# One block for a whole two-model, four-layer program: layer boundaries without loop, barriers and semaphore clears

## Chip, cores, metric

One NeuronCore of a Trainium2 chip. The metric is the device time of one execution in microseconds; smaller is better.

## What is computed

Two transformer-like blocks in sequence on one sequence of 256 tokens with 1024 features, each block two layers deep, all in f32:

```python
def first_block(x, ...):
    for l in range(DEPTH):                      # DEPTH = 2
        h = rms_norm(x, norm_mix_pre[l])
        mix = hybrid_mixer(h, w_in[l], ...)      # SSM, two softmax attentions, one top-k attention, gates
        x = x + rms_norm(mix, norm_mix_post[l])
        h = rms_norm(x, norm_ffn_pre[l])
        x = x + rms_norm(swiglu(h, w_ffn_in[l], w_ffn_out[l]), norm_ffn_post[l])
    return x

def second_block(x, mem, positions, ...):
    for l in range(DEPTH):
        h = rmsnorm(x, norm_mix[l])
        x = x + mixer_block(h, positions, w_in[l], ...)   # MLA, spatial gate, GLA, delta net, gates
        x = x + cross_attention(rmsnorm(x, norm_xattn[l]), rmsnorm(mem, norm_mem[l]), ...)
        x = x + squared_relu_mlp(rmsnorm(x, norm_mlp[l]), w_up[l], w_down[l])
    return rmsnorm(x, norm_final)
```

Every layer reads its own weights once; they are most of the data.

## The kernel before

`build` loads `x` and shared constants, then calls `first_block` and `second_block`. Tiles of the first have names with `a_`, of the second with `b_`. Each has a loop over its two layers that is executed on the chip (`nc.Fori`), so the program holds one copy of a layer's instructions for each block. In the loop stands one block (`nc.Block`) with one instruction stream for each engine, written out by hand: TensorE (PE), ScalarE (ACT), VectorE (DVE), GpSimd (POOL) and SyncE (SP), which issues every DMA. Engines meet only through semaphores.

A layer is a **stream of weight parts**, 87 in a layer of block 1 and 84 in one of block 2, most of 1 MB. For part `h` SP loads it into one of three slots of `ring`; ACT's `hi` (L707, L2198) rounds it to the matmul's input type into `whi`; DVE's `lo` (L923, L2462) writes the rest into `wlo`; and PE multiplies three times (lo by hi, hi by lo, hi by hi), at L400, L660 and L690 in block 1 and L1675, L1701, L1752 and L2181 in block 2. There are three slots of each: SP waits for `lo_ok` of part `h - 3`, ACT for PE to have used part `h - 3`.

The activations are split in the same way. Before each large product stands a **turn**: ACT squares `x` and sums, DVE makes the mean square, POOL the power -1/2, DVE scales `x` into `xm` (L937, L2476; the tile is named `probs`), PE turns it in 16 small products (L390, L1666), ACT writes `nhi` and DVE `nlo`, and then the first matmul of the product can start. It happens at the start of each layer (L710 on) and again in the middle (`norm_in(3, ...)` in block 1, `norm_in(6, ...)` and `norm_in(7, ...)` in block 2). At the end of a layer comes the down projection (`dn`, parts from `H_DN` or `H_DN2`); its result is normed and added to `x` in block 1 (`norm_out`, L946 and L948) and added in block 2 (`residual`, L2810).

At the end of a layer all engines meet, the semaphores are cleared and they meet again:

```python
            nc.all_engine_barrier()
            for s in sems:
                nc.gpsimd.sem_clear(s)
            nc.all_engine_barrier()
```

Only then does SP issue the next layer's loads: the parameter rows `par` (L346: 6 DMAs; L1604: 8), which PE turns (L581, L2123) and DVE copies to `parT`, the first parts (L356, L1636), and small tensors (L359: 4; `smalls`: 11 in block 2). Between the blocks stands another block of its own: SP loads `con2` and `pos`, DVE works out angles in a chain of dependent steps (L1566 to L1576), ACT takes their sine (L1583). After block 2 one more block does the last norm (L3007 to L3030), and a last one writes the output (L3063). At the start `build` waits for `x` and the constants, then `first_block` for `con1`, in blocks of their own.

Of the kernel before, what the change touches and what calls it, by code (L numbers as in the profile page):

```python
# [1 line left out]

# [14 lines left out]
P = 128  # L17
# [68 lines left out]

W1 = 512
# [52 lines left out]
def first_block(nc, ps, x, con, bfc, a):  # L140
    with ExitStack() as ctx:

        place = [29056]

        def at(name, shape, dt=F32, offset=None):

            size = int(np.prod(shape[1:])) * (2 if dt == BF16 else 4)
            if offset is None:
                offset = place[0]
                place[0] = (offset + size + 31) // 32 * 32  # L150
            return nc.alloc_sbuf_tensor_at("a_" + name, shape, dt, offset=offset)

        def sem(name):
            s = ctx.enter_context(nc.semaphore("a_" + name))
            sems.append(s)
            return s

        sems = []
        ident = con[:, C_ID:C_ID + P]
        ident_bf, maskT_bf, maskQ_bf = (bfc[:, i, :] for i in range(3))  # L160
        tri = con[:, C_U:C_U + NT * SEQ].rearrange("p (t l) -> p t l", t=NT)
        maskQ = con[:, C_MQ:C_MQ + P]

        con1 = at("con1", [P, N_CONST1])
        cos, sin = con1[:, C1_COS:C1_COS + SEQ], con1[:, C1_SIN:C1_SIN + SEQ]
        rot = con1[:, C1_ROT:C1_ROT + P]
        ring = at("ring", [P, SLOTS, PART])
        whi, wlo = at("whi", [P, SPLITS, PART], F32R), at("wlo", [P, SPLITS, PART], F32R)
        nhi, nlo = at("nhi", [P, KD, SEQ], F32R), at("nlo", [P, KD, SEQ], F32R)

        base = place[0]
        gates = at("gates", [P, 32, SEQ])
        hid = gates
        dump = at("dump", [P, NT, D], offset=base)
        xbcp = at("xbcp", [P, 8, SEQ + 4], offset=base)
        xbc = at("xbc", [P, 8, SEQ], offset=base + 8320)
        xd = at("xd", [P, 2, NT, W1], offset=base + 16512)
        y = at("y", [P, NT, W1], offset=base + 24704)

        base = place[0]
        ys = at("ys", [P, 4, 4, SEQ])
        rl = at("rl", [P, 4, 384], offset=base + 8192)
        hhi, hlo = (at(n, [P, SPLITS, 2 * SEQ], F32R, offset=base + i * 6144) for i, n in enumerate(("hhi", "hlo")))

        base = place[0]
        fq, fk, fv = at("fq", [P, 4, SEQ]), at("fk", [P, 4, SEQ]), at("fv", [P, NT, W1])
        dq, dk, dv = fq, fk, fv  # L190
        merged = at("merged", [P, KD, SEQ], offset=base)

        base = place[0]
        mq, mk, mv = at("mq", [P, 4, SEQ]), at("mk", [P, 4, SEQ]), at("mv", [P, NT, W1])
        sc8 = at("sc8", [P, 8, 384], offset=base + 4096)
        ahi, alo = (at(n, [P, 4, SEQ], F32R, offset=base + i * 4096) for i, n in enumerate(("ahi", "alo")))
        gpost2 = at("gpost2", [P, D], offset=base + 8192)
        probs = at("probs", [P, 8, SEQ])
        xm = probs[:, :, :].rearrange("p (t a) b -> p t (a b)", t=NT)  # L200

        base = place[0]
        pT = at("pT", [P, 8, SEQ])
        iqf = at("iqf", [P, 4, SEQ], offset=base)
        cb = at("cb", [P, 2, 384], offset=base + 4096)
        bhi, blo = (at(n, [P, 4, SEQ], F32R, offset=base + i * 4096) for i, n in enumerate(("bhi", "blo")))

        base = place[0]  # L210
        z = at("z", [P, NT, W1])
        gpost1 = at("gpost1", [P, D], offset=base)
        ffg = at("ffg", [P, 2, 2 * SEQ], offset=base)
        o = z
        rt = at("rt", [P, 2, SEQ])
        par, parT = at("par", [NPAR1, P]), at("parT", [P, NPAR1])
        small = at("small", [P, 4, 8])
        sel, nsel = at("sel", [P, 16], F32R), at("nsel", [P, 16], F32R)
        iw = at("iw", [P, NT, 4])
        sp = at("sp", [P, 6, NT * 16])  # L220
        lcat = at("lcat", [P, NT, P])
        asg = at("asg", [P, 16])
        cumS = at("cumS", [P, SEQ], F32R)
        ncum = at("ncum", [P, NT, 16])
        isc = at("isc", [P, 384])
        pen = at("pen", [P, 384], BF16)
        top8 = at("top8", [P, 8])
        nmx, rsum, rinv = at("nmx", [P, 2, 8]), at("rsum", [P, 2, 8]), at("rinv", [P, 8])
        ssq, msq, rstd = (at(n, [P, 5, 4]) for n in ("ssq", "msq", "rstd"))
        nhalf = at("nhalf", [P, 4])  # L230
        assert place[0] <= 229344, place[0]

        dst = dict(xbc=xbcp[:, :, 3:SEQ + 3], iqk=iqf, few=iqf[:, 2:4, :],
                   fq=fq, fk=fk, fv=fv, mq=mq, mk=mk, mv=mv, dq=dq, dk=dk, dv=dv, z=z)
        isct = [isc[:, 0:P], isc[:, P:3 * P]]
        pent = [pen[:, 0:P], pen[:, P:3 * P]]
        rlt = [rl[:, :, 0:P], rl[:, :, P:3 * P]]

        con1_in = sem("con1_in")
        par_in, small_in, gpost_in = sem("par_in"), sem("small_in"), sem("gpost_in")  # L240
        landed = [sem(f"landed{i}") for i in range(SLOTS)]
        hi_ok, lo_ok = sem("hi_ok"), sem("lo_ok")
        full, turn_ps, free_a, free_v = (sem(n) for n in ("full", "turn_ps", "free_a", "free_v"))
        par_ps, par_ok = sem("par_ps"), sem("par_ok")
        ssq_ok, msq_ok, rstd_ok = sem("ssq_ok"), sem("msq_ok"), sem("rstd_ok")
        xn_ok, x_ok, tr_ps, nhi_ok, nlo_ok = (sem(n) for n in ("xn_ok", "x_ok", "tr_ps", "nhi_ok", "nlo_ok"))
        conv_ok, silu_ok, init_ok = sem("conv_ok"), sem("silu_ok"), sem("init_ok")
        few_ps, spv, spe, rope_ok = (sem(n) for n in ("few_ps", "spv", "spe", "rope_ok"))
        lcat_ok, cum_ps, cum_ok = sem("lcat_ok"), sem("cum_ps"), sem("cum_ok")
        cb_ps, cb_ok, xs_ps, xs_ok = sem("cb_ps"), sem("cb_ok"), sem("xs_ps"), sem("xs_ok")  # L250
        dec_ps, dec_ok, sc_ok = sem("dec_ps"), sem("dec_ok"), sem("sc_ok")
        y_ps, y_free, yt_ok, yt_ps, yt_out = sem("y_ps"), sem("y_free"), sem("yt_ok"), sem("yt_ps"), sem("yt_out")
        ix_ps, ix_rl, isc_ok, pen_ok = sem("ix_ps"), sem("ix_rl"), sem("isc_ok"), sem("pen_ok")
        qk_ps, mx_ok, ex_ok, pt_ps = sem("qk_ps"), sem("mx_ok"), sem("ex_ok"), sem("pt_ps")
        pt_a, pt_v, o_ps, o_ok, ot_ps, ot_ok = (sem(n) for n in ("pt_a", "pt_v", "o_ps", "o_ok", "ot_ps", "ot_ok"))
        sig_ok, yh_ok, yl_ok = sem("sig_ok"), sem("yh_ok"), sem("yl_ok")
        pr_ps, pr_free, mg_ok, mh_ok, ml_ok = (sem(n) for n in ("pr_ps", "pr_free", "mg_ok", "mh_ok", "ml_ok"))
        out_used, mix_ps, half_used = sem("out_used"), sem("mix_ps"), sem("half_used")
        fg_free, fu_free, hh_ok, hs_ok, dn_ps = (sem(n) for n in ("fg_free", "fu_free", "hh_ok", "hs_ok", "dn_ps"))
        dch = sem("dch")  # L260

        def cols(src, l, c, n):
            return src[bass.ds(l, 1), :, c:c + n].rearrange("a (k p) c -> p (a k) c", p=P)

        def rows(src, l, r, k):
            return src[bass.ds(l, 1), r:r + k * P, :].rearrange("a (k p) c -> p (a k) c", p=P)

        def branch_rows(l, n, j):
            return a["w_branch"][bass.ds(l, 1), n].rearrange("a (k p) c -> p (a k) c", p=P)[:, :, 512 * j:512 * j + 512]

        H_GATE = N_IN1
        H_BR = H_GATE + N_GATE1
        H_OUT = H_BR + 8
        H_FIN = H_OUT + 4
        H_DN = H_FIN + 2 * (HID1 // 256)
        H_END = H_DN + KH1 // 2
        parts = [(8, n, lambda l, c=c, n=n: cols(a["w_in"], l, c, n)) for c, n, _ in IN1]
        parts += [(8, 256, lambda l, c=c: cols(a["w_gate"], l, 256 * c, 256)) for c in range(N_GATE1)]
        parts += [(4, 512, lambda l, n=n, j=j: branch_rows(l, n, j)) for n in range(4) for j in range(2)]  # L280
        parts += [(2, D, lambda l, i=i: rows(a["w_out"], l, 2 * i * P, 2)) for i in range(4)]
        parts += [(8, 256, lambda l, c=c, j=j: cols(a["w_ffn_in"], l, HID1 * j + 256 * c, 256))
# [25 lines left out]
        def last_fill(i):  # L308
            return filled["in", i, len(IN1[i][2]) - 1] if i < N_IN1 else filled["gate", i - N_IN1]
# [2785 lines left out]
```

## Time and profile before

| | us |
|---|---|
| median of 3 runs | 2556.69 (2553.71 to 2557.05) |
| the profiled execution, its own time | 2554.51 |
| its span, first to last instruction | 2552.4 |
| PE busy in the span | 2371.9 |
| DVE, ACT, POOL busy | 1431.7, 1093.0, 48.5 |
| mean granted TensorE clock | 0.968 |

The span is what the trace shows; the execution's own time is 2.1 us more. "Boundary" below is the stretch from the last matmul of one layer to the first full matmul of the next: the first is between the layers of block 1, the second between the blocks, the third between the layers of block 2.

### The profile page before, as it was taken

To read this page: it belongs to the slowest core of one execution; us is meant where nothing else is said; L and a number is where in the kernel's file an instruction comes from. 1 tells how busy PE (TensorE), PEld (TensorE's weight loads), DVE (VectorE), ACT (ScalarE), POOL (GpSimd) and SP (SyncE) were. 2 spreads that over 40 slices of the span, in tenths; PEclk is the share of its full clock that TensorE was granted. 3 is DMA by queue.
4 is the path that set the end of the run, shared out by engine and by line. 5 is a ranking of instruction groups with operands and counts; after the bars stand their busy time and mean duration, and the time that the engine had idled before them with its cause. 6 is when DMAs were issued, how large, how long until landed. Compare 5 with 4: busy or idle time off the path is not lost. (4 is left out here: it accounts for less than half of the span.)

```text
span 2552.4 us, 40497 instructions
## 1 busy us (share of the span) xinstructions
PE 2371.9 (93%) x17164; PEld 2216.8 (87%) x17164; DVE 1431.7 (56%) x1573; ACT 1093.0 (43%) x1356; POOL 48.5 (2%) x49
## 2 busy tenths in 40 slices
PE   6999998998799999899759999989987999998996
PEld 6988997997798899799659998979966999897985
DVE  6555457444655545644447867454545876744553
ACT  4534444333453354434246433543424643443442
POOL 0000000000000000000000000000000000000000
PEclk9999999999899999999979999999998999998998
DMA  6523355543743336555254434445526443444552
GB/s 201 159 83 110 114 191 165 180 169 114 200 139 93 102 114 198 165 168 197 92 161 125 126 100 146 158 149 165 183 98 188 130 119 100 158 140 148 182 194 78
DMA packets 300001, 370.32 MB, mean 145 GB/s; under 512 B 25006, under 2 KB 267300, under 8 KB 299812
## 3 DMA queue, kind: packets, MB, share of 16 engines
q1 hardware_dynamic: 299812, 367.62, 45.8%
q8 instruction: 140, 2.29, 0.4%
q14 instruction: 49, 0.40, 0.0%
HBM read 366.55 MB, written 1.05 MB: 144 GB/s over the span
## 5 line engine op out<-in xcount | busy, mean ns | idle before, releaser
L400 PE MATMUL ps<-a_nhi,a_wlo 128*128 128x256 f32 x1792 | 525.0, 293 | 12.7 <-DVE a_nlo L953 11.2
L400 PE MATMUL ps<-a_nlo,a_whi 128*128 128x256 f32 x1792 | 508.0, 284 | 0.0
L400 PE MATMUL ps<-a_nhi,a_whi 128*128 128x256 f32 x1792 | 507.9, 283 | 0.0
L923 DVE TENSOR_TENSOR a_wlo<-a_ring,a_whi 128x2048 fp32r<-128x2048 f32 x174 | 395.6, 2286 | 108.3 <-ACT a_whi L707 107.8
L2462 DVE TENSOR_TENSOR b_wlo<-b_ring,b_whi 128x2048 fp32r<-128x2048 f32 (+1 forms) x168 | 379.6, 2263 | 136.2 <-ACT b_whi L2198 136.0
L707 ACT CAST a_whi<-a_ring 128x2048 fp32r<-128x2048 f32 x174 | 331.1, 1905 | 195.3 <-PE ps L400 73.2
L1675 PE MATMUL ps<-b_nhi,b_wlo 128*128 128x256 f32 x1296 | 378.4, 292 | 16.1 <-DVE b_wlo L2462 8.5
L2198 ACT CAST b_whi<-b_ring 128x2048 fp32r<-128x2048 f32 (+1 forms) x168 | 316.2, 1884 | 165.8 <-PE ps L2181 77.4
L1675 PE MATMUL ps<-b_nlo,b_whi 128*128 128x256 f32 x1296 | 369.8, 285 | 0.0
L1675 PE MATMUL ps<-b_nhi,b_whi 128*128 128x256 f32 x1296 | 369.7, 285 | 0.0
L400 PEld LDWEIGHTS ps<-a_nhi,a_wlo 128*128 128x128 f32 x1792 | 345.3, 193 | 18.9 <-DVE a_wlo L923 12.2
L400 PEld LDWEIGHTS ps<-a_nlo,a_whi 128*128 128x128 f32 x1792 | 344.7, 192 | 2.5 <-issue 2.4
L400 PEld LDWEIGHTS ps<-a_nhi,a_whi 128*128 128x128 f32 x1792 | 344.2, 192 | 0.0
L1675 PEld LDWEIGHTS ps<-b_nhi,b_wlo 128*128 128x128 f32 x1296 | 251.9, 194 | 19.2 <-DVE b_wlo L2462 9.4
L1675 PEld LDWEIGHTS ps<-b_nlo,b_whi 128*128 128x128 f32 x1296 | 252.0, 194 | 0.9 <-issue 0.5
L1675 PEld LDWEIGHTS ps<-b_nhi,b_whi 128*128 128x128 f32 x1296 | 251.6, 194 | 0.0
L2181 PE MATMUL ps<-b_whi,b_hlo 128*128 128x512 f32 x256 | 99.6, 389 | 0.0
L2181 PE MATMUL ps<-b_wlo,b_hhi 128*128 128x512 f32 x256 | 99.6, 389 | 0.0
L2181 PE MATMUL ps<-b_whi,b_hhi 128*128 128x512 f32 x256 | 99.6, 389 | 0.0
L1244 DVE TENSOR_TENSOR a_gates<-a_ffg,ps 128x512 f32<-128x512 f32 x22 | 15.1, 688 | 142.5 <-PE ps L400 142.5
L775 ACT ACTIVATE a_probs<-ps,a_nmx 128x128 f32<-128x128 f32 (+1 forms) x96 | 39.3, 430 | 94.5 <-DVE a_nmx L1074 94.5
L421 PE MATMUL ps<-a_wlo,a_nhi 128*128 128x256 f32 x256 | 75.6, 295 | 0.0
(537 smaller groups left out, 4390.0 us busy)
## 6 DMA issues: line engine op xcount, KB each, us to landing
a_ring<-in_w_in SPq DMA_DIRECT2D x50, 1024.0 KB, 5.2
b_ring<-in_w_in SPq DMA_DIRECT2D x50, 1024.0 KB, 6.1
a_ring<-in_w_ffn_in SPq DMA_DIRECT2D x44, 1024.0 KB, 5.4
a_ring<-in_w_gate SPq DMA_DIRECT2D x32, 1024.0 KB, 5.3
b_ring<-in_w_up SPq DMA_DIRECT2D x32, 1024.0 KB, 5.5
b_ring<-in_w_down SPq DMA_DIRECT2D x32, 1024.0 KB, 5.0
a_ring<-in_w_ffn_out SPq DMA_DIRECT2D x22, 1024.0 KB, 5.0
a_ring<-in_w_branch SPq DMA_DIRECT2D x16, 1024.0 KB, 5.1
```

The costliest lines, as they stand in the source:

```text
L400: mm = T.matmul(out, w[:, k, c:c + P], x_[:, k, :], start=k == 0 and n == 0, stop=k == KD - 1 and n == 2)
L421: mm = T.matmul(b[:, t * size:(t + 1) * size], x_[:, k, t * P:(t + 1) * P], w[:, k, c:c + size], start=k == 0 and j == 0, stop=k == KD - 1 ...
L707: S.copy(part(whi, h), part(ring, h)).then_inc(hi_ok, 1)
L775: ins = S.activation(probs[:, s, 0:w], L[:, s, 0:w], ACT.Exp, bias=nmx[:, n % 2, s:s + 1], accum_out=rsum[:, n % 2, s:s + 1])
L923: V.tensor_tensor(part(wlo, h), part(ring, h), part(whi, h).bitcast(F32), ALU.subtract).then_inc(lo_ok, 1)
L1244: V.tensor_tensor(hid[:, 2 * c:2 * c + 2, :], ffg[:, c % 2, :].rearrange("p (b c) -> p b c", b=2), ps[:, 4 + c % 2, :].rearrange("p (b c) ...
L1675: mm = T.matmul(out, w[:, k, c:c + P], x_[:, k, :], start=k == 0 and n == 0, stop=k == KD - 1 and n == 2)
L2181: mm = T.matmul(ps[:, 4 + 2 * t + half, :], hidden_of(x_, i)[:, kk, t * P:(t + 1) * P], w[:, kk, half * 512:(half + 1) * 512], start=i + k ...
L2198: A.copy(part(whi, h), part(ring, h)).then_inc(hi_ok, 1)
L2462: V.tensor_tensor(part(wlo, h), part(ring, h), part(whi, h).bitcast(F32), ALU.subtract).then_inc(lo_ok, 1)
```

## The change

All engines' work is put into one block. Each layer becomes a `Stage`, and the engines run through four stages that are written out one after the other; there is no loop, no barrier between them and no clearing. Semaphores count on through the program: `Counting` adds what the earlier layers have given to every wait (`GAINED_1`, `GAINED_2`), and the two blocks share semaphores and the same addresses for `ring`, `whi`, `wlo`, `nhi`, `nlo`. At the end of a layer, `hi`, `lo` and SP go on with the first parts of the next layer; its `par` rows are loaded at part `H_DN + 1` and turned by PE in the down projection (`i == 6` or `i == 9`). The angles of block 2 are worked out by DVE at `H_DN + 6` of the layer before (`set_vector`), the sines by ACT at `H_DN + 8`. `x` is loaded in two halves, each with its semaphore; the last norm and the output go by halves, and `norm_final` is loaded during the last down projection.

The core of the diff, without the change of indentation:

```diff
+    def wait_ge(self, sem, n):
+        self.engine.wait_ge(sem, n + self.done[sem.name])
...
-        with nc.Fori(0, DEPTH) as l:
-            with nc.Block() as block:
...
+    def ends(l):
+        at_ = lambda sem, n: (sem, n + earlier(l, 0)[sem.name])
+        return Ends(split=[at_(lo_ok, H_END - 2 + i) for i in range(3)],
+                    used=[at_(*used[H_END - 3]), at_(*used[H_END - 2]), at_(dn_ps, 2)],
+                    x=[at_(x_ok, 3), at_(x_ok, 4)], hidden=at_(hs_ok, KH1 // 2))
...
+            elif prior is not None:
+                sp_.wait_for(*prior.split[h])
+            if h == H_DN + 1:
+                following.params(sp_.engine, following.layer)
+            if l == 0 and h == 1:
+                sp_.dma_start(con1[:, :], a["constants_1"]).then_inc(con1_in, 16)
...
-                    pe.wait_ge(par_in, 96)
-                    T.transpose(ps[:, 4, 0:NPAR1], par[:, :], ident[0:NPAR1, 0:NPAR1]).then_inc(par_ps, 1)
                     turned(0)
...
+            if i == 6:
+                pe.wait_ge(fu_free, KH1 // 2)
+                following.params_turn(pe.engine, following.layer, 4)
...
+        def hi(h):
+            if h < H_END:
+                split_hi(act.engine, l, h, prior)
+            elif following is not None:
+                following.split_hi(act.engine, following.layer, h - H_END, ends(l))
...
                     for t in range(NT):
+            act.wait_for(*(x_in[t] if prior is None else prior.x[t]))
                         squares(0, t, x[:, t, :])
+        if prior is None:
                     hi(0)
...
+            if i == H_DN + 6:
+                following.set_vector(dve.engine, following.layer)
+            if i == H_DN + 7:
+                following.params_out(dve.engine, following.layer, 4)
...
-            nc.all_engine_barrier()
-            for s in sems:
-                nc.gpsimd.sem_clear(s)
-            nc.all_engine_barrier()
...
                         if h == SLOTS - 1:
+                sp_.wait_for(*prior.hidden)
+                sp_.wait_for(init_ok, 2)
                             smalls()
...
+            if i == 9 and following is not None:
+                following.params_turn(pe.engine, following.layer, 2)
...
+        if following is None:
+            for t in range(NT):
+                sp_.wait_for(y_ok, t + 1)
+                sp_.dma_start(y.rearrange("a (t p) d -> p (a t) d", p=P)[:, t, :], x[:, t, :]).then_inc(y_done, 16)
```

How the instructions move on ACT at the second boundary. Before, from the last casts of block 1's layer to the first of block 2's (`a_hhi` is the hidden activation's rounded half, `b_trig` the sines):

```order
L707 CAST a_whi<-a_ring 128x2048 [waits a_landed2,a_half_used]
L905 CAST a_hhi<-a_gates 128x512 [waits a_fu_free]
L710 ACTIVATE a_dump,a_ssq<-ps 128x1024 [waits a_dn_ps] x2
L336 UNCONDITIONAL_BRANCH
L335 REGISTER_ALU [waits barrier_Pool_Activation_PE_DVE_SP_release]
L335 COMPARE_AND_BRANCH
L1580 UNCONDITIONAL_BRANCH
L1583 ACTIVATE b_trig<-b_lnp 32x256 [waits b_ang_ok]
L1584 ACTIVATE b_trig<-b_lnp 32x256
L1544 UNCONDITIONAL_BRANCH [waits b_trig_ok]
L1588 UNCONDITIONAL_BRANCH [waits barrier_Pool_Activation_PE_DVE_SP_release]
L2189 UNCONDITIONAL_BRANCH
```

and now:

```order
L804 CAST a_whi<-a_ring 128x2048 [waits landed2,half_used]
L1741 ACTIVATE b_trig<-b_tmp_148 32x256 [waits ang_ok]
L1742 ACTIVATE b_trig<-b_tmp_148 32x256
L1017 CAST a_hhi<-a_gates 128x512 [waits fu_free]
L2354 CAST b_whi<-b_ring 128x1536 [waits landed0,half_used]
L2354 CAST b_whi<-b_ring 128x1536 [waits landed1,half_used]
L818 ACTIVATE a_dump,a_ssq<-ps 128x1024 [waits dn_ps] x2
L2368 ACTIVATE b_dump,b_ssq<-x 128x1024 [waits x_ok] x2
L2374 ACTIVATE b_nhi<-ps,b_parT 128x256 [waits tr_ps,par_ok]
```

The branches and barrier waits are gone; the next block's first two casts stand ahead of the last squares of this one, and the squares of `x` follow on `x_ok` alone.

On DVE at the same place, now, the set-up chain of block 2 inside block 1's down projection:

```order
L1025 TENSOR_TENSOR a_wlo<-a_ring,a_whi 128x2048 [waits hi_ok]
L1720 MEMSET b_nhalf 128x8
L1721 MEMSET b_eps 128x1
L1722 MEMSET b_wg 128x128
L1724 CAST b_tmp_148<-b_pos 32x256 [waits con1_in]
...
L1734 TENSOR_SCALAR b_tmp_148<-b_tmp_148 32x256 [waits dch]
L1392 TENSOR_TENSOR a_hlo<-a_gates,a_hhi 128x512 [waits hh_ok]
L1025 TENSOR_TENSOR a_wlo<-a_ring,a_whi 128x2048 [waits hi_ok]
L2627 COPY b_parT<-ps 128x63 [waits par_ps]
```

`a_hlo` is what PE's next down-projection part waits for; the chain of ten dependent steps now stands ahead of it, where before it stood in a block of its own.

On SP (L128 is the helper that issues), now, what is issued between the last parts of block 1 and the fourth part of block 2:

```order
L128 DMA b_ring<-in_w_in 128x4x384 [waits lo_ok] x2
L128 DMA b_ring<-in_w_in 128x8x64 [waits lo_ok]
L128 DMA b_ring<-in_w_in 128x8x32 x2
L128 DMA b_sgw<-in_sg_w 128x4x128 [waits init_ok,hs_ok]
L128 DMA b_wuq<-in_mla_w_uq 128x2x384
...
L128 DMA b_lnp<-in_sg_ln_b 128x256
L128 DMA b_ring<-in_w_in 128x8x256 [waits lo_ok] x17
```

The order of the loads is that of before; their waits are now on the layer before (`lo_ok`, and `hs_ok` for the small tensors), not on a barrier.

## Rows read from the trace of the kernel before

**Rows 1.** The page: part 1 (busy time), part 3 (queue that brings instructions).

```profile
PE 2371.9 (93%) x17164; PEld 2216.8 (87%) x17164; DVE 1431.7 (56%) x1573; ACT 1093.0 (43%) x1356; POOL 48.5 (2%) x49
...
q8 instruction: 140, 2.29, 0.4%
```

**Rows 2.** Waits of PE: engine, line, on whom; total us, times, longest.

```profile
PE ps L2123 <- DMA b_par<-in_dn_conv: 60.3, 2, 37.1
...
PE ps L1675 <- DVE b_wlo L2462: 8.5, 4, 5.6
```

**Rows 3.** Timeline of PE, first boundary: start us, us, engine, line, operation [idle].

```profile
628.95 0.39 PE L690 MATMUL ps<-a_whi,a_hhi 128*128 128x512 f32 x1
...
646.49 0.41 PE L581 MATMUL ps<-con,a_par 92*128 92x92 f32 x1 [17.16 <-DMA a_par<-in_norm_ffn_pre]
...
655.89 0.55 PE L400 MATMUL ps<-a_nhi,a_wlo 128*128 128x256 f32 x1 [4.04 <-DVE a_nlo L953]
```

**Rows 4.** Timeline inside layer 1 of block 1, PE and DVE.

```profile
430.21 0.39 PE L660 MATMUL ps<-a_whi,a_nhi 128*128 128x512 f32 x1
...
434.75 1.23 DVE L948 TENSOR_TENSOR x<-x,a_probs 128x1024 f32<-128x1024 f32 x1
...
438.44 0.75 DVE L937 TENSOR_SCALAR a_probs<-x,a_rstd 128x1024 f32<-128x1024 f32 x1 [0.44 <-POOL a_rstd L1265]
...
442.39 0.36 PE L400 MATMUL ps<-a_nhi,a_wlo 128*128 128x256 f32 x1 [0.74 <-DVE a_nlo L953]
```

**Rows 5.** Timeline of PE and DVE, second boundary (block 1 to block 2).

```profile
1260.42 0.39 PE L690 MATMUL ps<-a_whi,a_hhi 128*128 128x512 f32 x1
...
1276.50 0.28 DVE L1566 CAST b_lnp<-b_pos 32x256 f32<-32x256 int32 x1 [3.76 <-DMA b_pos<-in_positions]
...
1279.96 0.28 DVE L1576 TENSOR_SCALAR b_lnp<-b_lnp 32x256 f32<-32x256 f32 x1
...
1302.70 0.41 PE L1701 MATMUL ps<-b_whi,b_nlo 128*128 128x384 f32 x1 [0.89 <-DVE b_nlo L2482]
```

**Rows 6.** Timeline of DVE and PE, third boundary.

```profile
1904.35 1.22 DVE L2810 TENSOR_TENSOR x<-x,ps 128x1024 f32<-128x1024 f32 x1 [1.50 <-PE ps L2181]
...
1932.20 0.66 PE L1701 MATMUL ps<-b_whi,b_nlo 128*128 128x384 f32 x1 [0.79 <-DVE b_nlo L2482]
```

**Rows 7.** Stretches (us; busy of PE, PEld, DVE, ACT, POOL; PEclk, DMA, GB/s), PE's timeline.

```profile
442.00:444.00 2.00, 1.61 (x13) 1.63 (x14) 2.00 (x6) 1.98 (x6) 0.00 (x0) 1.00 0.03 8
...
1722.21 0.55 PE L1675 MATMUL ps<-b_nhi,b_wlo 128*128 128x256 f32 x1 [3.00 <-DVE b_nlo L2482]
...
1728.00:1732.00 4.00, 4.00 (x34) 4.00 (x34) 0.49 (x1) 1.12 (x2) 0.00 (x0) 0.97 0.27 93
...
1936.00:1938.00 2.00, 2.00 (x12) 2.00 (x11) 1.62 (x2) 0.00 (x0) 0.00 (x0) 0.88 0.38 97
```

**Rows 8.** Timeline of the start: SP's DMA issues, DVE, PE.

```profile
6.97 0.50 DVE L3053 CAST bfc<-con 128x128 bf16<-128x128 f32 x3 [6.97 <-DMA x<-in_x]
...
11.32 0.37 SPq L346 DMA_DIRECT2D a_par<-in_norm_mix_pre  x1
...
14.01 2.41 SPq L356 DMA_DIRECT2D a_ring<-in_w_in  x3
...
24.38 0.55 PE L400 MATMUL ps<-a_nhi,a_wlo 128*128 128x256 f32 x1 [5.62 <-DVE a_nlo L953]
```

**Rows 9.** Timeline of the end: DVE, SP.

```profile
2529.43 1.22 DVE L2810 TENSOR_TENSOR x<-x,ps 128x1024 f32<-128x1024 f32 x1 [1.50 <-PE ps L2181]
...
2544.98 2.48 DVE L3023 SCALAR_TENSOR_TENSOR x<-x,b_rstd,b_probs 128x1024 f32<-128x1024 f32 x2 [1.50 <-DMA b_probs<-in_norm_final]
2547.95 0.39 SPq L3063 DMA_DIRECT2D out<-x  x1
```

**Rows 10.** Timeline of ACT and DVE near the end of layer 1.

```profile
613.05 1.91 ACT L707 CAST a_whi<-a_ring 128x2048 fp32r<-128x2048 f32 x1 [3.01 <-PE ps L690]
...
617.21 0.69 DVE L1253 TENSOR_TENSOR a_hlo<-a_gates,a_hhi 128x512 fp32r<-128x512 f32 x1
```

More of the change, by code:

```diff
@@ L1 @@
 from contextlib import ExitStack
+from dataclasses import dataclass
 import numpy as np
@@ L84, in column, with __init__, wait_for, dma_start @@
     return ap.broadcast_to([ap.shape[0], n])
+@dataclass
+class Ends:
+    split: list
+    used: list
+    x: list
+    hidden: tuple
+@dataclass
+class Stage:
+    layer: int
+    params: object
+    params_turn: object
+    params_out: object
+    set_vector: object
+    set_picks: object
+    set_scalar: object
+    split_hi: object
+    split_lo: object
+    sync: object
+    tensor: object
+    scalar: object
+    vector: object
+    gpsimd: object
+    ends: Ends
+class Counting:
+    def __init__(self, engine, done):
+        self.engine, self.done = engine, done
+    def wait_ge(self, sem, n):
+        self.engine.wait_ge(sem, n + self.done[sem.name])
+    def wait_for(self, sem, n):
+        self.engine.wait_ge(sem, n)
+    def dma_start(self, *args):
+        return self.engine.dma_start(*args)
@@ L3039, in build @@
         con_in, con_bf = (ctx.enter_context(nc.semaphore(n)) for n in ("con_in", "con_bf"))
-        out_done = ctx.enter_context(nc.semaphore("out_done"))
+        x_in = [(ctx.enter_context(nc.semaphore(f"x_in{t}")), 16) for t in range(NT)]
+        sems, n_chain = {}, [0]
+        stages = first_block(nc, ctx, sems, n_chain, ps, x, x_in, con, bfc, a)
+        stages += second_block(nc, ctx, sems, n_chain, ps, x, con, bfc, a, y)
+        first = stages[0]
+        run = [(s, stages[i - 1].ends if i else None, stages[i + 1] if i + 1 < len(stages) else None)
+               for i, s in enumerate(stages)]
         with nc.Block() as block:
```

5155 lines of the change are left out of this document (2623 added, 2532 removed).

## Prediction

> **What bounds the kernel now.** I began with the page. PE is busy 93% of the span [rows 1], and every other engine has slack, so the question is where PE stands still. The view of its waits answers that [rows 2]: its longest waits are for `b_par`, the parameter rows of a layer of block 2, 60.3 us in two waits. Those rows are loaded only after the barrier, so this is a layer boundary seen from PE. I then went through PE's timeline and noted every idle time above 0.4 us. Apart from some of about 1 us they lie at five kinds of place: the start, the three boundaries, the end, the norm in the middle of a layer, and a wait for `b_wlo` soon after a boundary. So the time is a dense stream of matmuls plus these gaps, and each gap can be priced from the timeline.
>
> The gaps, from the last matmul of a layer to the first full one of the next:
> - first boundary [rows 3]: 628.95 + 0.39 = 629.34 to 655.89, 26.55 us;
> - second [rows 5]: 1260.42 + 0.39 = 1260.81 to 1302.70, 41.89 us;
> - third [rows 6]: DVE's last addition to `x` starts at 1904.35, the first matmul at 1932.20, 27.85 us.
>
> **What a boundary costs without barriers.** Nothing has to be guessed here, since the middle of a layer in block 1 has the same chain: squares of the product, norm, addition to `x`, squares of `x`, norm, turn, `nhi`, `nlo`, matmul, with its weights split beforehand. From its last matmul (430.21 + 0.39 = 430.60) to the next at 442.39 it takes 11.79 us [rows 4]. From the end of the last addition to `x` (434.75 + 1.23 = 435.98) to the matmul it is 6.41 us [rows 4]. I take these as what remains.
>
> **The sum**, against the profiled execution's own time, 2554.5 us:
> - First boundary: the chain is the one of rows 4. 26.55 - 11.79 = 14.8 us saved.
> - Second: the same chain, with block 2's turn at its end. 41.89 - 11.79 = 30.1 us. The set-up of block 2 that stood here goes elsewhere, below.
> - Third: block 2 only adds to `x`; the addition ends at 1904.35 + 1.22 = 1905.57, and 6.41 us later, at 1911.98, the matmul can start. 1932.20 - 1911.98 = 20.2 us.
> - Weights behind a boundary: PE waits 8.5 us in four waits for `b_wlo` [rows 2], of which the largest, 5.6, and one of 2.0 stand behind the second and third boundary, where the fourth part was loaded after 11 small tensors. Now these loads stand before the boundary, some 10 us earlier than their use. 7.6 us.
> - Start: the first weight part is issued at 14.01 and PE's first full matmul comes 10.37 us later [rows 8]. Now the three loads of `x` and constants are issued at once from about 0.7 us, and the six `par` loads (11.32 to 14.01, so 0.45 us each [rows 8]) follow directly: 0.7 + 9 x 0.45 = 4.8 us for the first part, matmul at 4.8 + 10.4 = 15.2 instead of 24.38. 9.2 us. The other input is not later: `x` had landed by 6.97 [rows 8], and the norm and the turn of `x` fit in the 8 us that are left.
> - End: before, addition to `x` until 2529.43 + 1.22 = 2530.65, last scaling until 2544.98 + 2.48 = 2547.46, output issued at 2547.95, span end 2552.4 [rows 9]. Now the second half is squared, normed and scaled right behind its addition. From an addition's end to the scaling's start is 438.44 - 435.98 = 2.46 us [rows 4], one scaling is 1.24: 2530.65 + 2.46 + 1.24 = 2534.35, plus the 4.94 us from there to the end of the span as before, 2539.3. 13.1 us.
> - PE's three turns of `par` stood in idle time, and stand now in the middle of a down projection: 3 x 0.41 us [rows 3] on PE. -1.2 us.
> Together 93.8 us.
>
> **What is hidden.** DVE's chain for the angles lasts 1279.96 + 0.28 - 1276.50 = 3.7 us, with its memsets 4 us [rows 5]. It now stands ahead of an `a_hlo`. A part of the down projection lasts (629.34 - 613.05) / 3 = 5.43 us. With ACT's cast at 613.05, `a_hlo` is done at 617.90 [rows 10], while the matmuls that need it start two parts after 613.05, at 623.9. So DVE has 6 us to spare, and 4 us fit; it makes the delay good in the next parts, of whose 5.4 us it uses 3.0. If that cover is gone, the cost is at most 4 us, once. ACT's two sines are shorter and have the same cover. SP's additional loads (10, 6 and 8 small ones, 3 to 5 us of issuing at each boundary) stand ahead of a weight part that is loaded three parts, 16 us, before its use. The clears and barriers themselves were on POOL and in the idle time already counted. Waits of SP on `hs_ok` hold back only the small tensors and the fourth part, by less than one part.
>
> **The clock.** After an idle time the granted clock is at 0.50 (1.2 GHz) for a while, then 1.00 (2.4 GHz). At the third boundary it is 0.88 over 1936 to 1938 [rows 7], so it rose at about 1936.5: 4.3 us at half speed, 2.1 us lost; I take as much for the other two, 6.3 us in all. What the shorter gaps will cost is open, since the rows differ: after the 11.8 us gap in block 1 the clock is 1.00 from the first matmul on (442 to 444), while after the like gap in block 2 it is 0.97 only from 1728 on and the matmuls began at 1722.21 [rows 7], so 5.9 us at half speed, 2.9 us lost. The bounds for each boundary are 0 and 2.9; I take the middle, as neither row is nearer to all three: 3 x 1.45 = 4.3. Net gain 2.0 us.
>
> The Trainium skill, "TensorE: Matmul & The Clock Gate", section "HAM oscillation — how this bites in real kernels", says that an idle gap between bursts of matmuls takes the clock back to half, so that each burst starts cold. By this rule all three boundaries would pay in full, and the sum would be 4.3 us worse than mine; the row of 442 to 444 does not agree with it, that of block 2 does.
>
> Sum: 93.8 + 2.0 = 95.8, so 2554.5 - 95.8 = 2458.7 us. The median of the runs stands 2.2 us above the profiled execution; the forecast for the median is thus between 2458.7 and 2460.9, and I give **2459.5**.
>
> **Rivals.**
> - Every burst starts cold, 2463.8 us: the mechanism is the idle time of 8 to 12 us that is left at each boundary; it decides if the clock has fallen when the first matmul comes. For it speaks the gap in block 2, against it the one in block 1, whose chain the first two boundaries share. This is the case that the Trainium skill, "TensorE: Matmul & The Clock Gate", would have.
> - The work that crosses the boundaries gets in the way: the chain on DVE makes a part late (4 us), the 11 small loads hold the fourth part back at two boundaries as long as today (7.6 us), and the three groups of `par` loads delay a weight part by their issue (24 x 0.45 = 11 us). In full 23 us are given back, about 2482 us. Rows 10 speak against it, with 6 us of slack per part where the additions are 4.
> - The boundaries don't close as written, because some wait counts on what comes late (a slot, a semaphore of the layer before): at all three boundaries about half of the 65 us stays, 2492 us. The order of the instructions on ACT and DVE speaks against it.
> - Slower than before: the program is twice as long, since no layer's code is used twice. The queue for instructions brought 140 packets with 2.29 MB [rows 1]. If the longer program made PE wait for its instructions, at each such packet, the price that decides is 95.8 / 140 = 0.7 us per packet; at 1 us each it gives 2554.5 - 95.8 + 140 = 2599 us. Against it: PE's timeline shows no idle time of that kind in a layer's 600 us, where it too runs straight on, and the packets are already as many as the instructions executed, not as those in the program.
>
> **How the numbers follow.** Something over 0.2% (5 us) is what a measurement of this kernel can tell from no change. My forecast has a chance of 0.6, cold bursts 0.2, the crossing work 0.12, boundaries half open 0.05, slower 0.02; some 0.01 is left for no change. So faster 0.97, same 0.01, slower 0.02. The range: at the low end all boundaries are warm (4.3 us), the two norms in block 2 too because their phase has moved (2 x 2.9), and half-size transfers at start and end save 1 us each, 2447.6. At the high end everything is cold (4.3), the first part lands behind `x` and constants (2.2 us: 6.97 plus the 5.2 us from issue to landing instead of 10.0), and the wait of 5.6 us stays: 2471.6; a little of the crossing work makes it 2474. The rest of it and the other rivals lie outside.
>
> **What would show it.** The profile of the changed kernel should have: gaps of 11.5 to 12 us at the first two boundaries and 7.5 to 8 at the third, ended by `nlo`, not by a DMA; no wait of 5.6 us for `b_wlo`; the first full matmul at 15 to 16 us; 10 us from the last matmul to the end; PE busy the same within 10 us; down projections without idle time on PE. I would be wrong if a gap is ended by `par` or by a landing part, if PE waits for `b_wlo` or `a_hlo` in a down projection, or if small idle times without a releaser are spread over the stream.

## The result, and the profile after

| | before | changed |
|---|---|---|
| median of the runs, us | 2556.22 (4 runs) | 2452.61 (2452.03 to 2454.24, 4 runs) |
| ratio, 95% interval | | 0.9595 [0.9583, 0.9606] |
| profiled execution, own time | 2554.51 | 2452.11 |
| its span | 2552.4 | 2450.2 |
| PE busy in the span | 2371.9 | 2364.6 |
| PE idle (span less busy) | 180.5 | 85.6 |

The forecast was 2459.5 us with a range of 2447.6 to 2474: right in direction and inside the range, 6.9 us too high. The last two lines of the table carry the reading: PE executes the same 17164 matmuls and now idles 94.9 us less; being busy with them takes 7.3 us less, most of it because fewer of them run at half speed (below).

The page after, the first line, part 1 and the instruction queue of part 3:

```profile
span 2450.2 us, 38959 instructions
...
PE 2364.6 (97%) x17164; PEld 2210.0 (90%) x17164; DVE 1430.4 (58%) x1564; ACT 1090.3 (44%) x1353; POOL 49.8 (2%) x50
...
q8 instruction: 136, 2.23, 0.4%
```

The waits of PE after (engine, line, on whom; total us, times, longest), against [rows 2]:

```profile
PE ps L486 <- DVE a_probs L1078: 24.1, 4, 7.5
PE ps L1822 <- DVE b_probs L2656: 20.7, 4, 7.3
PE ps L463 <- DMA a_par<-in_norm_ffn_pre: 8.1, 1, 8.1
...
PE ps L1831 <- DVE b_wlo L2621: 0.9, 2, 0.5
```

No wait for `b_par` is left (60.3 us before), and of the 8.5 us for `b_wlo` 0.9. What leads now is the norm's own chain, at the boundaries and in the middle of each layer: PE waits for `x` to be scaled (`probs`) before it can turn it.

PE's timeline at the start and the three boundaries (start us, us, engine, line, operation [idle]):

```profile
15.38 0.55 PE L496 MATMUL ps<-a_nhi,a_wlo 128*128 128x256 f32 x1 [1.19 <-DVE a_nlo L1094]
...
627.43 3.67 PE L486 MATMUL ps<-con,a_probs 128*128 128x128 f32 x16 [7.18 <-DVE a_probs L1078]
631.88 0.55 PE L496 MATMUL ps<-a_nhi,a_wlo 128*128 128x256 f32 x1 [0.78 <-DVE a_nlo L1094]
...
1244.88 3.28 PE L1822 MATMUL ps<-con,b_probs 128*128 128x128 f32 x16 [7.27 <-DVE b_probs L2656]
1249.30 0.41 PE L1857 MATMUL ps<-b_whi,b_nlo 128*128 128x384 f32 x1 [1.15 <-DVE b_nlo L2662]
...
1845.29 3.44 PE L1822 MATMUL ps<-con,b_probs 128*128 128x128 f32 x16 [3.44 <-DVE b_probs L2656]
1849.72 0.41 PE L1857 MATMUL ps<-b_whi,b_nlo 128*128 128x384 f32 x1 [0.99 <-DVE b_nlo L2662]
```

The last matmul of a layer ends where the idle time of the turn begins: 627.43 - 7.18 = 620.25, so the first boundary takes 631.88 - 620.25 = 11.63 us; the second 1249.30 - 1237.61 = 11.69, the third 1849.72 - 1841.85 = 7.87. They were 26.55 [rows 3], 41.89 [rows 5] and about 27.9 [rows 6].

DVE and SP at the end, against [rows 9]; PE's last matmul ends at 2441.55, the span at 2450.2:

```profile
2441.59 1.22 DVE L2991 TENSOR_TENSOR x<-x,ps 128x1024 f32<-128x1024 f32 x1 [1.50 <-PE ps L2338]
...
2445.83 1.28 DVE L3178 SCALAR_TENSOR_TENSOR x<-x,b_rstd,b_probs 128x1024 f32<-128x1024 f32 x1 [0.44 <-POOL b_rstd L3194]
...
2445.42 2.08 SPq L128 DMA_DIRECT2D out<-x  x2
```

The clock after the first, the second and the third boundary (stretches: us; busy of PE, PEld, DVE, ACT, POOL; PEclk, DMA share, GB/s), against [rows 7]:

```profile
631.50:633.50 2.00, 1.62 (x7) 1.65 (x8) 2.00 (x6) 2.00 (x5) 0.00 (x0) 0.50 0.00 0
633.50:635.50 2.00, 2.00 (x11) 2.00 (x11) 2.00 (x3) 1.23 (x1) 0.00 (x0) 0.50 0.00 0
635.50:637.50 2.00, 2.00 (x14) 2.00 (x14) 2.00 (x2) 0.00 (x0) 0.00 (x0) 0.71 0.04 6
...
1249.00:1251.00 2.00, 1.70 (x10) 1.73 (x11) 2.00 (x6) 2.00 (x5) 0.00 (x0) 1.00 0.00 0
...
1849.50:1851.50 2.00, 1.78 (x10) 1.81 (x11) 2.00 (x7) 2.00 (x5) 0.00 (x0) 1.00 0.00 0
```

At one boundary of three the first full matmuls are cold (at 1.2 GHz, from 631.88 to 636.6); behind the other two they run at 2.4 GHz. But the clock had fallen at all three. The turn that comes first ran at 0.50 throughout behind the first boundary, and it starts at 0.50 behind the second and the third boundary too, and there the clock rises while the turn's 16 products are all that PE does:

```profile
1245.00:1247.00 2.00, 2.00 (x10) 2.00 (x11) 0.78 (x2) 0.00 (x0) 0.14 (x1) 0.50 0.00 0
...
1247.00:1249.00 2.00, 1.16 (x8) 0.92 (x6) 0.72 (x2) 1.66 (x5) 0.00 (x0) 0.84 0.00 0
...
1845.40:1847.40 2.00, 2.00 (x10) 2.00 (x11) 0.78 (x2) 0.00 (x0) 0.15 (x1) 0.50 0.14 50
```

### The profile page after: what moved, and what is told of

It is laid out like the page before. It is cut to its first block, busy times and chain, and to the rows that moved or that the text cites. A ratio compares the mean times of both kernels' runs of the same rounds, so it can differ in the third digit from the quotient of the medians.

```text
span 2450.2 us, 38959 instructions
## 1 busy us (share of the span) xinstructions
PE 2364.6 (97%) x17164; PEld 2210.0 (90%) x17164; DVE 1430.4 (58%) x1564; ACT 1090.3 (44%) x1353; POOL 49.8 (2%) x50
## 4 chain that ended last, share of the span: by engine, by line
PE 94%; DVE 3%; ACT 1%; issue 1%; POOL 0%; DMA 0%; SPq 0%; POOLq 0%; ACTq 0%; DVEq 0%
PE ps L496 27%; PE ps L1831 21%; PE ps L2338 7%; PE ps L788 5%; PE ps L1842 4%; PE ps L517 4%; PE ps L741 4%; PE ps L1908 3%; PE ps L628 2%; PE ps L1891 2%; PE ps L755 1%; PE ps L663 1%; PE ps L2131 1%; PE ps L2117 1%; PE ps L2130 1%; DVE b_wlo L2621 1%
## 5 line engine op out<-in xcount | busy, mean ns | idle before, releaser
L1831 PEld LDWEIGHTS ps<-b_nhi,b_wlo 128*128 128x128 f32 x1296 | 249.6, 193 | 11.1 <-issue 9.1
L2393 ACT ACTIVATE b_gates<-ps 128x512 f32<-128x512 f32 x32 | 19.1, 597 | 128.1 <-PE ps L1831 128.1
```

Source lines behind the costliest of these rows:

```text
L1831: mm = T.matmul(out, w[:, k, c:c + P], x_[:, k, :], start=k == 0 and n == 0, stop=k == KD - 1 and n == 2)
```

## The experiments

All kernels but e5, e10 and e11 are the changed kernel with one or more pieces of the change undone or made larger. They ran in several groups on different chips, each beside the kernel before, whose medians were 2556.2 to 2558.0 us; so the ratio is the fairer comparison between groups, and a difference of medians under 2 us says little. Three numbers are read of each: the median, and PE's idle and busy time in the profiled execution (span less part 1's PE, as above), since the busy time moves with the clock from one execution to the next and the idle time does not.

| run | median, us | ratio to before, 95% | PE idle | PE busy |
|---|---|---|---|---|
| changed kernel | 2452.61 | 0.9595 [0.9583, 0.9606] | 85.6 | 2364.6 |
| e1 meeting at each boundary | 2459.19 | 0.9617 [0.9601, 0.9633] | 89.0 | 2369.6 |
| e2 and the clears | 2487.51 | 0.9730 [0.9714, 0.9746] | 120.1 | 2364.5 |
| e3 parts split late | 2453.48 | 0.9597 [0.9581, 0.9613] | 86.0 | 2365.0 |
| e4 parts loaded late | 2477.39 | 0.9687 [0.9671, 0.9703] | 103.1 | 2373.3 |
| e5 PE kept busy in gaps | 2444.30 | 0.9562 [0.9546, 0.9578] | 51.1 | 2392.0 |
| e6 parameter rows late | 2459.95 | 0.9622 [0.9606, 0.9638] | 90.8 | 2367.7 |
| e7 angles three times | 2459.54 | 0.9619 [0.9603, 0.9635] | 90.2 | 2368.5 |
| e8 last gain late | 2454.51 | 0.9600 [0.9584, 0.9616] | 88.0 | 2364.8 |
| e9 = e2 + e4 + e6 + e8 | 2518.28 | 0.9846 [0.9831, 0.9861] | 145.2 | 2372.2 |
| e10 changed kernel again | 2453.83 | 0.9592 [0.9578, 0.9607] | 85.5 | 2366.7 |
| e11 e5 and shorter waits | 2436.36 | 0.9528 [0.9515, 0.9541] | 45.0 | 2388.3 |
| e12 start undone | 2460.42 | 0.9624 [0.9608, 0.9640] | 93.2 | 2364.0 |

### The meeting and the clears

e1 puts each stage into its own `nc.Block`; SyncE issues the next layer's first three parts at the end of the stage before. e2 adds the meetings and clears under `if n`:

```diff
-        with nc.Block() as block:
+        for n, (stage, prior, following) in enumerate(run):
+            if n:
+                nc.all_engine_barrier()
+                for _ in range((76, 198, 122)[n - 1]):
+                    nc.gpsimd.sem_clear(con_in)
+                nc.all_engine_barrier()
+            with nc.Block() as block:
```

> One nc.Block for each of the four layers, so that all engines meet at each of the three boundaries; nothing is cleared, and all work that the change sends across a boundary (first weight parts loaded and split, parameter rows loaded and turned, angles) is still done before the meeting. Theory A (a boundary cost before what was queued behind the meeting, not the meeting): the squares of the first half of x start 1.2 us later, after the second half's addition, and a meeting takes 1 to 2 us; 3 to 5 us for each boundary, 2461 to 2467 us, the gaps on PE 15 to 16 us, 15 to 16 and 11 to 12 instead of 11.6, 11.7 and 7.9. Rival B (the meeting and the jump in the code cost most of the 14 us that lay between the last addition to x and ACT's next instruction at the third boundary): over 10 us for each, 2482 us or more.

> The kernel of e1 with as many semaphore clears on POOL and a second barrier at each boundary as before (76, 198 and 122 clears, all of one semaphore that is no longer used, so that the counts go on). Theory A: of the 14 us between the last addition to x and ACT's next instruction at the third boundary before, 3 to 5 were the meeting, and some 9 the 122 clears, 0.075 us each; so 396 clears cost 30 us more than e1, about 2494 us. Rival B (the clears are cheap): within 5 us of e1.

The first boundary, PE's timeline in e1 and in e2:

```profile
629.62 3.67 PE L491 MATMUL ps<-con,a_probs 128*128 128x128 f32 x16 [8.48 <-DVE a_probs L1083]
```

```profile
635.20 3.67 PE L491 MATMUL ps<-con,a_probs 128*128 128x128 f32 x16 [14.80 <-DVE a_probs L1083]
```

A meeting lengthens the idle time by 8.48 - 7.18 = 1.3 us, and by 1.3 at each of the other two. Most of that is what the squares of the first half of `x` lose by starting behind the second half's addition: they last 1.04 us, and by ACT's timeline they start 0.3 us after that addition ends (626.22, 626.53), so the meeting itself takes 0.3. The expected 3 to 5 us was too much, and the median lies below the expected range. The clears and the second meeting cost 14.80 - 8.48 = 6.3 us here and, by the same rows, 14.9 and 9.5 us at the others: (14.9 - 6.3) / (198 - 76) = 0.070 us for each clear, and 6.3 - 76 x 0.070 = 1.0 us for the second meeting. So of the 31.1 us of idle time between e1 and e2 (28.3 in the median) some 28 are 396 clears in a row on POOL, and 3 the three second meetings. The kernel before cleared some more than that: by its source block 2's list has 132 semaphores, not 122, 0.7 us more at each of two places; and at its second boundary the clears stood in two groups, with two meetings each. Rival B of e1 is out, and so is rival B of e2.

### What was loaded and split behind the meeting

In e3 `hi` and `lo` end with the layer, and the next one calls `hi(0)` behind its squares, `lo(0)` behind `norm_in` and `hi(1)` behind `nhi`:

```diff
-            elif following is not None:
-                following.split_hi(act.engine, following.layer, h - H_END, ends(l))
...
-        if prior is None:
-            lo(0)
+        lo(0)
```

e4 is e3 and one more wait of SyncE:

```diff
                 sp_.wait_for(*prior.split[h])
+                sp_.wait_for(*prior.x[1])
```

In e6 (without e3 and e4) PE's turn and DVE's copy of `par` stand at the start of the next layer, and SyncE:

```diff
-            if h == H_DN + 1:
-                following.params(sp_.engine, following.layer)
...
+            if h == SLOTS - 1 and prior is not None:
+                sp_.wait_for(*prior.x[1])
+                params(sp_.engine, l)
```

> No barrier; the first parts of the next layer are loaded ahead as in the change, but ACT and DVE round and split them only in the next layer, after the squares and after the scaling of x. Theory A (this work fits in the chain's idle time on its engines): ACT is idle from the end of the squares for 3 us, DVE from the scaling to the first nlo for 2.3 us, and the two operations last 1.9 and 2.3 us; 0 to 1 us for each boundary, 2452 to 2456 us. Rival B (splitting ahead is a large part of the gain): 1.9 + 2.3 us for each boundary, 2465 us.

> As e3, and SyncE also issues the next layer's first loads only when both halves of x are added to; the parameter rows are still loaded ahead. Theory A: the first part lands 5.2 us after its issue, then 1.9 + 2.3 us for the split, so that PE starts 9.5 to 10 us after the last addition instead of 6.6; 3 to 4 us for each boundary and some wait for a fourth part behind block 2's small tensors, 2462 to 2470 us. Rival B (loads are covered by the norm's chain): under 1 us for each boundary beyond e3.

> Only the parameter rows of the next layer are loaded behind the last addition to x, after the first three weight parts, and turned by PE and copied by DVE there; the constants and angles of block 2 are still ahead. Theory A: 6 or 8 loads of 0.45 us each and 2.1 us to land, then PE's turn of them ahead of the turn of x: 4.9 to 5.8 us after the addition, where the turn of x starts now after 2.2; 2.8, 3.7 and 3.7 us, 2462 us. Rival B (they fit in the norm's chain): under 1 us for each boundary, 2455 us or less.

e3: 0.4 us of idle time; the split fits into ACT's and DVE's own idle time, as expected of theory A. e4: PE's timeline at the first boundary and behind the second:

```profile
637.22 0.55 PE L497 MATMUL ps<-a_nhi,a_wlo 128*128 128x256 f32 x1 [4.87 <-DVE a_nlo L1090]
...
1275.69 0.39 PE L1827 MATMUL ps<-b_nhi,b_wlo 128*128 128x256 f32 x1 [4.02 <-DVE b_wlo L2617]
```

`a_nlo` is named, but it is late because it stands behind the late `wlo` on DVE. The first matmul comes 4.1 us later here, 3.0 and 2.6 at the others, and the fourth part is late again behind block 2's small tensors (4.0 and 2.6 us): 16.3 of the 17.5 us of idle time. That is theory A, but the median rose by 24.8 us and not by 10 to 18: in the profiled execution PE was also busy 8.7 us longer with the same matmuls, since more of them ran at half speed behind the longer waits (1257 to 1263, 1275 to 1280, 1870 to 1874 and 1886 to 1891), which the expectation had left out. e6: 5.2 us of idle time; the first matmul came 1.4, 2.0 and 2.8 us later, each less than expected, and why less was not tested.

### The cover of the work that was moved into the down projection

```diff
+        for _ in range(3):
             link(V.tensor_copy(ang, pos[64:96, :]))
             ...
```

> The chain for the angles is worked out three times over at its place in the last down projection of block 1 (same result), 7 us more on DVE in one piece. By the slack of the prediction (6 us, of which the chain takes 4) the hidden activation's low half comes 5 us late once: 2457 us, and an idle time of PE of about 5 us near 1215. Rival B (the cover is larger, several parts deep): 2452 to 2453 us, no idle time.

```profile
1219.42 0.76 PE L788 MATMUL ps<-a_whi,a_hlo 128*128 128x512 f32 x1 [4.71 <-DVE a_hlo L1392]
```

The slack of 6 us that the prediction worked out from [rows 10] holds: 4 us of chain are free, and 11 us (1207.63 to 1218.54) cost 4.7 us of idle time. The median is 6.9 us up and not 4.4 as expected: the matmuls behind the wait ran at half speed until 1225.5, some 2.6 us lost by their spacing.

### The two ends of the program

e8 loads `norm_final_2` only on `x_ok`; e12 lets SyncE wait for `x`, load `con1`, wait for it, and only then issue `par`.

> Only the gain of the last norm is loaded behind the last addition to x, as before, where the change loads it in the last down projection; the halves stay. It lands 3.9 us after its issue (2541.11 to 2544.98 before): the first scaling starts at 2446.7 instead of 2444.1 and the second right behind it, 2.2 us in all: 2454.3 us. Of the 14.3 us that the end became shorter the rest was then barriers, the clears, and halves in place of the whole. Rival B: the load is hidden behind the squares, 0.

> The start alone undone: SyncE waits for both halves of x, loads the constants of block 1 and waits for them, and only then issues the parameter rows and the first weight part; no barrier. Theory A (the start's 9.0 us are these two waits): x lands at about 7.2, the constants some 2.4 us after their issue, six rows of 0.45 us, so the first weight part is issued at 12.6 and the first full matmul comes 10.4 us later, at 23 instead of 15.4; 2460 us. Rival B (most of it was the ends of two blocks and the jumps between them): 18 us or earlier, 2455 us.

e8: 2.4 us of idle time, 1.9 us in the median. e12: the first full matmul at

```profile
22.66 0.55 PE L500 MATMUL ps<-a_nhi,a_wlo 128*128 128x256 f32 x1 [3.33 <-DVE a_nlo L1098]
```

instead of 15.38, 7.3 of the 9.0 us by which the start became shorter; what the other 1.7 us are was not tested. Both are theory A.

### Do the pieces add up?

> e2, e4, e6 and e8 together: at each boundary a meeting, the clears, a meeting, and behind them the parameter rows, the first weight parts and their splitting; the last gain behind the last addition. The angles and constants of block 2 stay ahead, start and halves at the end stay as changed. Theory A (the four pieces stand one behind the other and add up): 2452.6 + 34.9 (e2) + 24.8 (e4) + 7.3 (e6) + 1.9 (e8) = 2521.5 us, within 4; what is then left to the 2556.2 of before is the start (9.0), the clears and meetings ahead of the last norm (about 12) and the set-up of block 2 in a block of its own (the rest, 13). Rival B (they overlap: a part that lands late hides the parameter rows): 2512 us or less.

Page of e9, first line and part 1:

```profile
span 2517.4 us, 39462 instructions
...
PE 2372.2 (94%) x17164; PEld 2217.3 (88%) x17164; DVE 1430.4 (57%) x1564; ACT 1088.8 (43%) x1353; POOL 48.8 (2%) x50
```

In PE's idle time they add up: e2 34.5 + e4 17.5 + e6 5.2 + e8 2.4 = 59.6 us, and e9 has 145.2 - 85.6 = 59.6. That it is the same to 0.1 us is partly luck: the first two boundaries are 1.0 and 0.7 us longer than the sum of the pieces there, and the waits for `b_wlo` behind them 0.8 us shorter. The median is 3.2 us below the sum of medians, inside the expected 4; that is the busy time, which does not add up (e9's is 2372.2, where e4's alone is 2373.3). With e12's 7.6 us, 67.2 of the 94.9 us of idle time are accounted for by runs. The other 27.7 us lie, by the timelines of e9, e12 and before, mainly at the second boundary (33.6 us in e9, 41.9 before, with the block that set block 2 up and two more meetings), at the third (23.9 us in e9, 27.9 before; ACT loaded its table there before, 1.28 us, and not in e9) and at the end (some 12 us: blocks, clears and norm of both halves at once); the first boundary (0.8), the waits for `b_wlo` (1.8) and the start (1.7) hold the rest. These were not undone one by one, so their split is read, not shown, and what the loop itself cost was not tested.

### The clock

e5 adds, in front of each turn of `x` that PE waits for:

```diff
+        def warm(bank, n):
+            for _ in range(n):
+                T.matmul(ps[:, bank, 0:384], bfc[:, 0, :], bfc[:, :, :].rearrange("p a b -> p (a b)"),
+                         start=True, stop=True)
...
+        warm(3, 38)
         turned(0)
```

The first boundary in e5: PE's timeline, then the stretches behind it.

```profile
619.49 6.35 PE L470 MATMUL ps<-bfc 128*128 128x384 bf16 x38
626.83 2.29 PE L491 MATMUL ps<-con,a_probs 128*128 128x128 f32 x16 [0.99 <-DVE a_probs L1086]
630.52 0.36 PE L501 MATMUL ps<-a_nhi,a_wlo 128*128 128x256 f32 x1 [1.40 <-DVE a_nlo L1102]
```

```profile
626.00:630.00 4.00, 2.19 (x16) 1.71 (x16) 2.06 (x6) 1.45 (x5) 0.99 (x1) 1.00 0.00 0
630.00:632.00 2.00, 1.48 (x12) 1.50 (x13) 2.00 (x6) 2.00 (x6) 0.00 (x0) 1.00 0.00 0
632.00:634.00 2.00, 2.00 (x18) 1.99 (x17) 2.00 (x3) 1.39 (x1) 0.00 (x0) 1.00 0.00 0
```

The clock is 1.00 through the whole boundary. The turn of 16 takes 2.29 us instead of 3.67, and the matmuls behind it run at full speed (12 and 18 in 2 us, against 7 and 11). 8.3 us in the median, 10 expected; left were stretches at 0.50 at the start (16 to 18.8) and behind the norm in the middle of both layers of block 2 (1654 to 1657, 2252.7 to 2258), where PE waited 3.6 us for `nlo` after the turn with nothing to do. Rival B is out. PE's busy and idle times of this run don't compare with the others', because the added products count as busy.

> The changed kernel itself once more, on this chip and beside the others. If the low stretches of the clock after the gaps are a fixed thing of each place, the first boundary is followed by 4 us at half speed again, the second and third by none. If they are not: other places show them, and the sum over the program stays between 5 and 11 us of matmul time. Time 2452.6 within 1.5 us.

In e10 the idle time is the same to 0.1 us and the busy time is not. Behind its boundaries (first, then second):

```profile
632.00:634.00 2.00, 1.10 (x9) 0.88 (x8) 1.87 (x5) 2.00 (x7) 0.00 (x0) 1.00 0.00 0
1248.00:1250.00 2.00, 1.47 (x5) 1.50 (x6) 2.00 (x6) 2.00 (x6) 0.00 (x0) 0.50 0.00 0
1250.00:1252.00 2.00, 2.00 (x8) 2.00 (x7) 2.00 (x3) 0.54 (x1) 0.00 (x0) 0.50 0.00 0
```

Now the second boundary is cold and the first warm; the third is warm again, the start is warm where it was cold, and the norm in block 1's first layer is cold where it was warm. By the spacing of the matmuls (estimated as below) the cold bursts behind waits lose 6.9 us in the one execution and 8.2 in the other, inside the expected 5 to 11. At the boundaries the turn starts at 0.50 in both. So with these waits it is a matter of the execution, and not of the place, whether the clock has risen by the first full matmul. Nor is it the length of the gap: before the change PE waited 37.1 us at the second boundary, the turn ran at 0.50, and the first full matmul, at 1302.70, at 1.00:

```profile
1299.00:1301.00 2.00, 2.00 (x11) 2.00 (x10) 1.22 (x1) 0.28 (x1) 0.00 (x0) 0.50 1.06 313
...
1302.60:1304.60 2.00, 1.90 (x11) 1.93 (x12) 2.00 (x6) 2.00 (x5) 0.00 (x0) 1.00 0.87 246
```

### A version that beats both

e11 is e5 with 6 more such products ahead of the first matmul, 22 instead of 26 ahead of the turn of block 2's up projection, and in block 2:

```diff
-            pe.wait_ge(*((nlo_ok, 16) if i < 2 else (up_free, i - 1)))
+            if i:
+                pe.wait_ge(*((nlo_ok, 16) if i < 2 else (up_free, i - 1)))
...
+                if first and k % 2 == 0:
+                    pe.wait_ge(nlo_ok, first + k // 2)
...
-        lo(H_UP + 1)
         norm_in(7, 9, x)
+        lo(H_UP + 1)
```

> e5, and two waits of block 2 shortened: the first part of the up projection waits for its activations two at a time and not for all eight (PE idle 3.6 us ahead of it in e5, 1.3 in the like place of block 1), and DVE splits the next weight part behind the norm's scaling and not ahead of its mean square (0.9 us). In both layers of block 2. Theory A: 2 x (2.3 + 0.9) = 6.4 us, and 2.6 us of half speed behind the two waits go as well (1.43 and 2.67 us in e5's stretches, of which the turn's part stays): 2436 us. Rival B (the other half of the chain, ACT's casts of 0.38 us each, sets the end): 2442 us.

```profile
1650.88 0.35 PE L1848 MATMUL ps<-b_nhi,b_wlo 128*128 128x256 f32 x1 [1.99 <-DVE b_nlo L2683]
...
2245.06 0.36 PE L1848 MATMUL ps<-b_nhi,b_wlo 128*128 128x256 f32 x1 [1.98 <-DVE b_nlo L2683]
```

2436.36 us, as expected: 7.9 us less than e5 and 16.2 less than the changed kernel. The wait was 3.63 in e5 and is 1.99 (1.3 expected); the granted clock is 1.00 in every stretch of 2 us in which PE has work. What each of the four edits gives was not tested apart.

## Why the prediction was right, and where it was off

| term | predicted, us | measured, us |
|---|---|---|
| first boundary | 14.8 | 26.55 - 11.63 = 14.9 |
| second | 30.1 | 41.89 - 11.69 = 30.2 |
| third | 20.2 | 20.0 |
| weights behind a boundary | 7.6 | 8.5 - 0.9 = 7.6 |
| start | 9.2 | 24.38 - 15.38 = 9.0 |
| end | 13.1 | 23.0 - 8.65 = 14.4 |
| PE's turns of `par` | -1.2 | -1.1 (0.41 + 0.36 + 0.36, busy in these gaps before) |
| sum | 93.8 | 95.0 (PE idle by the page: 94.9) |
| clock | 2.0 | 7.3 (PE busy) |

- **Boundaries**: pricing what would remain by the like chain in the middle of a layer [rows 4] was right within 0.2 us at all three places. It needed no price for a barrier, and would have gone wrong with one: e1 and e2 show that the barriers are nearly free and the clears are not.
- **End**: the step "plus the 4.94 us from there to the end of the span as before" was too long by 1.8 us: the last half's output needs 3.1 us from the scaling's end (it is half the size; no run shows that this is why). The norm ahead of it takes 3.02 us, not 2.46.
- **Start**: 9.0 for 9.2, but by two errors that cancel. The first part was issued at 4.32 and not at 4.8, and the first full matmul came 11.1 us later and not 10.4, since the part landed later (ACT's cast starts at 10.23).
- **What is hidden**: right. Behind the start no wait for `a_hlo`, `par` or a landing part stands in the profile (at the start PE waits for `par` until 8.11), and e7 found the edge of the slack where it was expected.
- **The clock** is the term that was mis-sized, and with 5.3 us most of the miss. The losses here are estimates from the spacing of the full matmuls: 0.213 us at half speed and 0.119 at full for 128x256, 0.32 and 0.17 for 128x384. "I take as much for the other two, 6.3 us in all" was wrong at the second boundary, which was warm before the change (1302.60 above): the boundaries lost 3.8 us before. "The bounds for each boundary are 0 and 2.9; I take the middle ... 3 x 1.45" left 4.3 us; it was 2.1 us, at one of three (631.88 to 636.6). So their net gain was 1.7 us, and that it is near the forecast 2.0 is luck. What the sum put at nothing is larger: the cold burst behind the 5.6 us wait for `b_wlo`, which went with the wait (2.3 us, 1320.38 to 1325.5 before), and the two norms in the middle of block 2, which lost 1.6 us each where they had lost 2.7 and 2.3. With 0.2 us at the start that is 6.0 of the 7.3 us; the rest, in the turns and elsewhere, is not split. The low end of the range named the norms ("because their phase has moved"). As e10 shows, an execution of the same kernel can lose 2.1 us more; a sum made from one trace cannot be better than this.
- **Rivals**: "every burst starts cold" did not happen as it was priced, with all three boundaries paying in full. But its question, "if the clock has fallen when the first matmul comes", was not what decided: the clock had fallen at each of the three, and whether it rose again during the turn made the difference. The Trainium skill, "TensorE: Matmul & The Clock Gate", section "HAM oscillation — how this bites in real kernels", has each burst behind such a wait start cold; the trace agrees for the turns (0.50 at all three), and not for the full matmuls behind them (cold at one of three, and at another one in e10). The crossing work, the half-open boundaries and the instruction delivery showed nothing: the instruction queue brought 136 packets instead of 140 [rows 1], although no layer's code is used twice.

## What to carry to other kernels

To price the removal of a seam between stages, look for the same chain where there is no seam, and take its length as what remains; the pieces of the seam then need no price of their own. Split the span into PE idle and PE busy in every trace that you compare: in idle time these experiments added up within 1 us at each place, while the busy time of the same matmuls moves by up to 9 us with the clock. If PE is cold behind its waits, products of constants into a free bank during the wait can be worth more than a microsecond each: 8.3 us for the seven waits of 3.4 to 7.5 us and the start here.

## What the hardware did that was not expected

- A semaphore clear on POOL costs 0.070 us in a row of them; 396 of them cost 28 us of idle time, where the six meetings beside them cost 3.4 (e1) and about 3 (e2).
- A meeting of all five engines added no more than 1.3 us to a gap in which they all waited for the same addition anyway; ACT's next instruction came 0.3 us after that addition.
- Behind a wait of 37.1 us the granted clock was back at 1.00 by the first full matmul, 4.8 us after the wait, and behind one of 7.2 us it was not: in between PE had done nothing but turns, at both places.
- At the start of the changed kernel the granted clock is given as 1.00 from 15 us on, but the matmuls are as slow as in a cold stretch until 18.7 (12 in 2 us, then 19):

```profile
17.00:19.00 2.00, 2.00 (x12) 2.00 (x11) 1.72 (x3) 2.00 (x2) 0.00 (x0) 1.00 1.06 366
19.00:21.00 2.00, 2.00 (x19) 2.00 (x18) 2.00 (x2) 0.64 (x1) 0.00 (x0) 1.00 0.35 119
```

  So near a trace's start the count of matmuls is the better clock.
- The turns of f32 tiles run at full speed when PE was kept busy before them: 16 in 2.29 us against 3.67.
